# Expert stage of a two-layer diffusion step: 512-column gate/up loads in two slots, and a down product in three fp32r passes

## What is computed

```python
def swiglu(x, wg, wu, wd):
    return (jax.nn.silu(x @ wg) * (x @ wu)) @ wd

def moe(x, w_router_l, wg, wu, wd):
    logits = (x @ w_router_l).astype(jnp.float32)
    top_v, top_i = lax.top_k(logits, TOP_K)
    gates = jax.nn.softmax(top_v, axis=-1)
    ...
    for e in range(N_EXPERTS):
        out = out + combine[..., e:e + 1] * swiglu(x, wg[e], wu[e], wd[e])
```

## Time and profile before

| | us |
|---|---|
| median of 3 runs | 2133.07 |
| lowest and highest | 2130.3 and 2135.24 |
| the profiled execution (its span) | 2131.6 |
| PE busy | 1916.8 (90%) |
| DVE busy | 909.3 (43%) |
| ACT busy | 675.0 (32%) |

### The profile page before, as it was taken

One profiled execution on the slowest core, in us unless ns is written; L12 is line 12 of the kernel. 1 busy time (PEld: TensorE's weight loads), 2 busy tenths in 40 slices (PEclk: granted clock), 3 DMA queues, 4 the chain that ended last, 5 costly groups with the idle time before them and its releaser, 6 DMA issues.

```text
span 2131.6 us, 20882 instructions
## 1 busy us (share of the span) xinstructions
PE 1916.8 (90%) x7660; PEld 1289.0 (60%) x7661; DVE 909.3 (43%) x1352; ACT 675.0 (32%) x1026; POOL 109.5 (5%) x93
## 2 busy tenths in 40 slices
PE   6999898899996798999779898989999898999793
PEld 2444444788886796554656565656666566666562
DVE  0303602433335724442545555555555544333454
...
PEclk9999998999998897557679999999999999999897
DMA  9565659333334423001559999999999997544792
GB/s 298 188 214 182 198 203 358 121 119 119 99 119 93 125 80 99 1 1 59 178 173 303 324 325 314 333 315 313 307 326 301 322 299 261 178 148 159 235 297 110
DMA packets 359072, 436.78 MB, mean 205 GB/s; under 512 B 32332, under 2 KB 311528, under 8 KB 358968
## 3 DMA queue, kind: packets, MB, share of 16 engines
...
## 4 chain that ended last, share of the span: by engine, by line
PE 81%; DVE 9%; issue 5%; ACTq 2%; ACT 2%; DMA 1%; DVEq 0%; POOL 0%; POOLq 0%
PE ps L1601 33%; PE ps L1618 15%; PE ps L1525 7%; PE ps L1566 5%; PE ps L1498 4%; PE ps L1629 4%; PE ps L1668 3%; PE ps L1731 3%; PE ps L1707 2%; DVE split L1219 2%; PE ps L1580 2%; PE ps L1680 2%; ACTq L821 2%; DVE ring_split L1283 1%; DVE extra_split L1283 1%
## 5 line engine op out<-in xcount | busy, mean ns | idle before, releaser
L1601 PE MATMUL ps<-split,hi_x 128*128 128x512 f32 (+1 forms) x2304 | 693.4, 386 | 25.0 <-issue 20.2
L1219 DVE TENSOR_TENSOR split<-ring,split 128x1024 fp32r<-128x1024 f32 (+1 forms) x432 | 469.1, 1131 | 103.3 <-ACT split L829 101.4
L1601 PEld LDWEIGHTS ps<-split,hi_x 128*128 128x128 f32 x2304 | 419.8, 193 | 110.6 <-issue 33.2
L1601 PE MATMUL ps<-split,lo_x 128*128 128x512 f32 (+1 forms) x1152 | 438.8, 381 | 0.0
L829 ACT ACTIVATE split<-ring 128x1024 fp32r<-128x1024 f32 (+1 forms) x432 | 389.3, 977 | 52.7 <-issue 35.2
L1618 PE MATMUL ps<-ring,work 128*128 128x512 f32 x792 | 357.9, 593 | 3.7 <-DVE work L1252 3.7
L857 ACT ACTIVATE work<-ps 128x256 f32<-128x256 f32 (+1 forms) x144 | 52.8, 367 | 691.8 <-PE ps L1601 691.7
L1246 DVE TENSOR_TENSOR work<-work,ps 128x256 f32<-128x256 f32 (+1 forms) x144 | 57.4, 399 | 479.1 <-ACT work L857 432.1
L1601 PEld LDWEIGHTS ps<-split,lo_x 128*128 128x128 f32 x1152 | 220.8, 192 | 42.1
L1618 PEld LDWEIGHTS ps<-ring,work 128*128 128x128 f32 x792 | 147.9, 189 | 150.6 <-issue 142.8
L1525 PE MATMUL ps<-ring,cond 128*2 128x256 f32 x576 | 128.0, 383 | 9.6 <-DMA ring<-in_w_mod_dram 9.6
...
## 6 DMA issues: line engine op xcount, KB each, us to landing
ring<-in_moe_w_gate_dram SPq DMA_DIRECT2D x80, 1024.0 KB, 7.4
ring<-in_moe_w_up_dram SPq DMA_DIRECT2D x80, 1024.0 KB, 9.9
ring<-in_moe_w_down_dram SPq DMA_DIRECT2D x80, 1024.0 KB, 5.1
ring<-in_w_mod_dram SPq DMA_DIRECT2D x36, 1024.0 KB, 7.4
mod_extra<-in_w_mod_dram SPq DMA_DIRECT2D x12, 1024.0 KB, 6.9
ring<-in_w_qkv_dram SPq DMA_DIRECT2D x6, 2048.0 KB, 8.9
ring<-in_w_in_dram SPq DMA_DIRECT2D x5, 2048.0 KB, 10.3
ring<-in_ffn_w_gate_dram SPq DMA_DIRECT2D x10, 1024.0 KB, 7.7
```

The source lines that it names most:

```text
L1219: dve.tensor_tensor(low, raw, high.bitcast(F32), ALU.subtract).then_inc(lo_ok, 1)
L1601: ins = pe.matmul(ps[:, 0, 0:2 * w], xt(c_), split[:, j % 2, part, c_, 0:2 * w], start=(c_ == 0 and n == 0), stop=(c_ == KC - 1 and n == 2))
```

## The change

Everything before the experts keeps its order, except as listed. In the experts:

- **Loads.** `E_WIDTH` makes five slabs of 512 columns and one of 256. Gate and up of a slab are 2 MB each, with 2 KB per row; down is one 2 MB load. There are two slots (`e_raw`, `e_draw`) instead of three. The SP queue gates the load of slab j with `used(i, j-1)`: PE must have finished the gate/up products of slab j-2 for both tiles (`e_gu`). Down of slab j waits for the down products of slab j-2, and that of slab 1 for the end of the round before.
- **Steps.** The 12 steps stay, two to a slab (`expert_step`).
- **Low parts over the raw weights.** `e_lo` has the address of `e_raw`: DVE writes the low part over the raw value. So the slot stays taken until PE has multiplied with it. The high part goes to `e_hi`. The pieces are fewer in number, but the instructions have the same size (128x1024, ten full steps) and number (four on each engine).
- **Down product.** `expert_down_of`: 12 fp32r matmuls in a full step (6 in a half step) in place of 8 records. For it ACT writes the high part of the down weights (`expert_down_high`, one instruction of 128x2048) and DVE the low part (`expert_down_low`, 128x2048), and the hidden values are split too: ACT copies the high part out of PSUM and DVE subtracts. ACT's copy and its split of the down weights are new in its order; on DVE the subtraction takes the place of the copy, and the split of the down weights comes at the end of each step.
- **Around it.** SP waits for the end of the attention's v products before it loads `w_o`. The first expert's slab 0 is loaded then, slab 1 after the output product, and its down slabs after the squares of norm 3. ACT and DVE split the first down step right behind that of gate/up step 0, ahead of the row copies. The small routing tiles move to `route`; `final_g` is loaded at the end of the last round.

```diff
+AREA = 4096
+E_WIDTH = [2 * SF] * (D_FF // (2 * SF)) + [D_FF % (2 * SF)]
+E_PIECES = 2
...
+            e_raw = first.enter_context(nc.sbuf_tensor("e_raw", [P, 2, 2, AREA], F32))
+            e_draw = first.enter_context(nc.sbuf_tensor("e_draw", [P, 2, AREA], F32))
...
+        e_lo = sb("e_lo", [P, 2, 2, AREA], F32R)
+        e_dlo = sb("e_dlo", [P, 2, AREA], F32R)
+        e_hi = sb("e_hi", [P, 2, KC, 2 * SF], F32R)
+        e_dhi = sb("e_dhi", [P, 2, 2, D], F32R)
...
@@ block.sync @@
+            sp.wait_ge(v_ps, 4 * TILES)
             for f in range(2):
                 fill(F_O + f, slab(F_O + f), w_o[0].rearrange(kview, p=P)[:, :, f * 512:(f + 1) * 512])
...
+            def used(i, j):
+
+                for k in range(2):
+                    sp.wait_ge(e_gu[k], i * STEPS + (STEPS + 2 * j))
+
+            gate_up_fill(0, 0)
+            sp.wait_ge(*last_use(F_O))
+            sp.wait_ge(*last_use(F_O + 1))
+            gate_up_fill(0, 1)
+            sp.wait_ge(ssq_ok, 4 * TILES)
+            down_fill(0, 0)
+            down_fill(0, 1)
...
             with sp.Fori(1, rounds) as i:
                 e = sp.snap(i % EXPERTS, min_val=0, max_val=EXPERTS - 1)
...
-                for j in range(STEPS):
-
-                    sp.wait_ge(lo_ok, i * (PIECES * STEPS) + PIECES * (STEPS + j - SLOTS + 1))
+                for j in range(len(E_WIDTH)):
+
+                    used(i, j - 1)
                     gate_up_fill(e, j)
...
+                    if j == 1:
+
+                        sp.wait_ge(done[0], i + 1)
+                        sp.wait_ge(done[1], i + 1)
+                    elif j == 0:
+                        sp.wait_ge(down_used, i * (STEPS - 1) + (STEPS - 2))
                     else:
...
+                        sp.wait_ge(down_used, i * (STEPS - 1) + (STEPS - 1 + 2 * (j - 1)))
+                    down_fill(e, j)
@@ block.scalar, moe_round @@
-                    for j in range(STEPS):
+                    for s in range(STEPS):
+                        n = WIDTH[s]
                         for k in ks:
-                            silu(k, j, i * STEPS + (STEPS + j), moe_buf)
-                        if j + 2 < STEPS:
-                            split_ahead(j + 2, i)
+                            act.wait_ge(e_gu[k], i * STEPS + (STEPS + s + 1))
+                            act.activation(e_silu[:, 0:n], ps[:, 0, 0:n], ACT.Silu).then_inc(silu_ok, 1)
+                            if k == ks[-1] and s + 2 < STEPS:
+                                expert_high(s + 2, i)
+                            act.wait_ge(h_turned, nth(ks, i, s, k))
+                            act.activation(h_split[:, 0, 0:n // P, :],
+                                           ps[:, 1, 0:n].rearrange("p (f t) -> p f t", t=P), ACT.Copy).then_inc(ht_hi, 1)
+                        if s:
+                            act.wait_ge(down_used, i * (STEPS - 1) + (STEPS - 1 + s))
...
+                        if s + 1 < STEPS:
+                            expert_down_high(s + 1, i)
+                        if s == STEPS - 1:
+                            turned_in(0, i + 2)
+                        if s + 2 >= STEPS:
                             with act.If(left > 1):
-                                split_ahead(j + 2 - STEPS, i + 1)
+                                expert_high(s + 2 - STEPS, i + 1)
+                                if s + 1 == STEPS:
+                                    expert_down_high(0, i + 1)
@@ block.vector, moe_round @@
+                            dve.wait_ge(silu_ok, nth(ks, i, s, k))
+                            dve.tensor_tensor(e_prod[:, 0:n], e_silu[:, 0:n], ps[:, 0, n:2 * n],
+                                              ALU.mult).then_inc(h_ok, 1)
                             if ahead:
-                                split_ahead(j + 2, i, range(0, PIECES // 2))
-                            hidden_turned(k, j, i * STEPS + (STEPS + j), moe_buf)
+                                expert_low(s + 2, i, range(0, E_PIECES // 2))
+                            dve.wait_ge(ht_hi, nth(ks, i, s, k))
+                            dve.tensor_tensor(h_split[:, 1, 0:n // P, :], ps[:, 1, 0:n].rearrange("p (f t) -> p f t", t=P),
+                                              h_split[:, 0, 0:n // P, :].bitcast(F32), ALU.subtract).then_inc(ht_ok, 1)
                             if ahead:
-                                split_ahead(j + 2, i, range(PIECES // 2, PIECES))
-                        if j == STEPS - 1:
+                                expert_low(s + 2, i, range(E_PIECES // 2, E_PIECES))
+                        if s + 1 < STEPS:
+                            expert_down_low(s + 1, i)
...
@@ block.tensor @@
+            def expert_down_of(s, k):
+
+                n = WIDTH[s] // P
+                low = expert_rows(e_dlo, s)
+                for f in range(n):
+                    high = e_dhi[:, s % 2, f, :]
+                    for m, (part, wt) in enumerate(((0, high), (0, low[:, f, :]), (1, high))):
+                        for hf in range(2):
+                            ins = pe.matmul(ps[:, 2 + 2 * k + hf, :], h_split[:, part, f, :],
+                                            wt[:, hf * 512:(hf + 1) * 512], start=(s == 0 and f == 0 and m == 0),
+                                            stop=(s == STEPS - 1 and f == n - 1 and m == 2))
```

317 lines of the change are left out of this document (172 added, 145 removed).

## The result

The changed kernel takes **2201.6 us** (median of 4 runs, 2197.9 to 2204.4) against 2134.2 us of the kernel before on the same chip: 1.031 times as long, 95% interval 1.029 to 1.033. The forecast was 2184 in a range from 2148 to 2228. The profiled execution has a span of 2196.1 us, against 2131.6 before.

What follows compares the result with a forecast made beforehand. PE was taken to set the pace within a round, transfers close behind. PE's gain -61, late slabs +42, round ends +62 and clock +9 sum to +52 us on 2131.6: 2184 us, range 2148 to 2228.

Steps and rivals of the forecast that it cites:

- PE's gain of 61 us: Experts' down product in three passes: a full step gains 0.62 us, a tile-round 6.8 us, nine tile-rounds 61 us.
- Rival (4): Split low operand slows PE, or the three passes are no faster here: 61 us less gain, 2245 us; chance 0.05.
- ACT's and DVE's operations: Full expert step: ACT's work 6.6 us, DVE's 7.7 us; both fit into 8.57 us and alone cost nothing.
- The late slab: Slabs 2 and 4 of one-tile rounds land 13.3 us after request, cost 3.1 us each: +42 us over seven rounds.
- The turn of step 11: Round's end: PE waits 7.1 us instead of 0.68, since ACT must split the next expert's slab 0 first.
- The turn of step 0: Next round's start: PE idles 10.3 us instead of 8.07, from late DVE work and 7.5 us of DVE's idle time.
- ACT's own way (2.3 idle, table load, Silu: 3.64 us): Round's start: ACT's path from DVE's result copy to step 0's Silu, taken as lower bound for the restart.
- the clock's term: Round ends: two long PE waits a round lower the granted clock for the next product, 7 x 1.25 = +9 us.
- Rival (1): Round's end: DVE's idle 9.18 us comes from full load queues and shrinks to 2.4 us; 2155 us; chance 0.12.
- Rival (3): ACT's longer one-tile branch brings exposed idle times of 6 to 9 us once more a round: 2226 us; chance 0.16.
- Rival (2): Slabs land in time, in under 10.4 us, and the restart is short too: faster, 2115 us; chance 0.08.
- Before and after the rounds: First down slab makes ACT wait 1.6 us without effect; later `w_o` and `final_g` loads are hidden: cost nothing.

## Why the prediction was right, and where it was not

**PE's gain of 61 us: right by the step.** Steps of 5.48 + 2.80 + 0.22 us against the 8.57 I counted with; the split low operand costs nothing. Rival (4) falls. Over the whole program PE's busy time fell by 44 us (1916.8 to 1872.9); more of the products ran at a lower granted clock (0.91 instead of 0.96 in the round shown above). And this gain is no number that stands by itself. With resident loops on the old slots the passes gain 19 us (2100.1 to 2081.4), and 14 of them come in the one round with two tiles (213.3 to 199.0 us from store to store). The five whole one-tile rounds take 107.1 us each with the new product and 107.7 with the old: PE works 4.5 us less in each and idles 4.0 more, since ACT's and DVE's added splits lengthen the round's end. On the wide slabs the same passes cost 36 us (2127.5 to 2163.6).

**ACT's and DVE's operations: right.** A 128x2048 copy of down takes 1.92 us (1.9), its low part 2.28 (2.25).

**The late slab: right in mechanism, size off by a little.** Landing 13.2 us after the request (1224.90 to 1238.1) against 13.3. The first late slab costs 1.26 + 1.67 = 2.9 us, the second 0.40 + 1.65 = 2.05, against 3.1 each: 35 us in all instead of 42. Slab 4 is as late as slab 2 (ACT waits 4.47 and 4.46 us for them). It costs less since PE comes to the down product later there: it turns gathered tokens first (1273.28, 1.03 us), which I hadn't counted. The next expert's slab 0 takes 14.0 us (1299.79 to 1313.81). For slab 3 I had 1.6 us of lateness and left out the 0.4 of the Silu; ACT waits 1.01 us for it, and it costs nothing, as said.

**The turn of step 11: right.** 8.13 us against 7.1; ACT waits 4.21 us for slab 0 there.

**The turn of step 0: the size nearly right, the reason wrong.** I had 10.3 us, made of late work on DVE and 7.5 us of DVE's idle time taken over as it was. It is 11.7 to 11.8 us, and DVE isn't last: ACT is. From the end of DVE's result copy to its Silu it takes 10.3 us (1331.86 to 1342.18), where I had 3.64 as its way and as the lower bound. The step that failed is "ACT's own way (2.3 idle, table load, Silu: 3.64 us)" as something that the change leaves alone. ACT's loop went from 230 to 373 instructions and is fetched again in every round.

**What 2184 lacks.** 17.6 us. By the terms and for seven rounds: the turn of step 0 is 1.4 us longer than forecast, +10; that of step 11 1.0 us longer, +7; the late slabs 1.2 us less, about -8. PE's work in a one-tile round fell by 4.3 us (105.1 to 100.8, the mean of five) where the gain less the clock's term was 5.6, +9. That is 18 us, an estimate, since the first round and the round with two tiles went their own way. A one-tile round takes 126.1 us where I had some 123.

**Rival (1), a short restart when the queues are idle: falls.** From some 1336 us on the queues moved 0 to 30 GB/s, and the idle time was longer than ever. **Rival (3), more restarts because ACT's code grew,** had 0.16, and it is what happened: I priced it at 42 us, and moving both loops gave 37 back. It did not come once more at another place, as I wrote, but in the same place on another engine, so that it took the place of the restart of DVE that my sum had already. That is why the sum came out close, and it is luck: the 7.5 us of restart in it stand for another cause on another engine. **Rival (2)** falls with the landing time.

**What I treated as given** was the 9.18 us of DVE in the earlier trace rows: an idle time for nothing, in 5 of 7 rounds. PE's wait for it was the largest that came back in every one-tile round of the kernel before. It was neither the jump nor the queues, but a loop of 333 instructions in an unlucky place; 77 idle instructions ahead of it take 29 us off the kernel.

**Before and after the rounds: right.** ACT waits 2.18 us for the first down slab (1.6 forecast) and nothing comes of it; the stretches up to 1020 us agree in both kernels, and so does the time behind the last store, 32.0 and 32.3 us.

**Two small slips.** In the earlier trace rows PE and the transfers are both high from slice 22 on, not 20. And the bounds add up to 2147 to 2212, not 2150 to 2215.
